# A fifth room for expert weights, and all of an octet's gathers in one pair: one buffer of gathered tokens in place of two

## The reference, cut to what matters

```
s = sigmoid(x @ router_w)                     # 64 experts, 8 chosen per token
shared = (silu(x @ sw1) * (x @ sw3)) @ sw2    # one shared expert for all tokens
for each expert e, on the tokens that chose it:
    xe = x[tok]                               # gather
    h  = silu(xe @ w1[e]) * (xe @ w3[e])      # 1024 -> 256, "gate" and "linear" product
    out[tok] += gate * (h @ w2[e])            # 256 -> 1024, "down" product, scatter
x = layer_norm(alpha * x + shared + out)
```

## Time and profile before

| | |
|---|---|
| median of 3 timed runs | 1344.71 us (1343.71 to 1345.81) |
| profiled execution | 1348.52 us, its span 1346.7 us |
| granted TensorE clock, mean | 0.999 |
| busy share of the span: PE, DVE, ACT, POOL | 97%, 35%, 23%, 6% |
| moved by DMA | 462.00 MB, mean 343 GB/s |
| chain that ended last | PE 77%, DMA 19%, DVE 2% |
| expert stage, layer 0 and layer 1 | about 178 to 637 us and 846 to 1304 us |

### The profile page before, as it was taken

The page is one execution under the profiler, slowest core; times in us unless marked ns, Lnnn a source line. Parts: engine busy times, 40 slices in busy tenths (PEclk is TensorE's granted clock), DMA queues, the critical chain, the costliest instruction groups (busy, mean ns, idle before and its releaser), DMA issues.

```text
span 1346.7 us, 23086 instructions
## 1 busy us (share of the span) xinstructions
PE 1303.1 (97%) x9730; PEld 750.1 (56%) x9730; DVE 475.4 (35%) x791; ACT 310.7 (23%) x747; POOL 81.0 (6%) x93
## 2 busy tenths in 40 slices
PE   9999999999999899998999999999999999999998
PEld 4555665555555455554498457555555545555544
DVE  1584532333332323323511246232332323333344
ACT  1244322121221221111210234222222221112112
POOL 2443100000000000000100021000000000000000
PEclk9999999999999999999999999999999999999999
DMA  9820679999999999999764527799999999999992
GB/s 305 305 97 32 250 299 419 420 420 421 421 421 420 421 420 422 420 420 385 244 229 147 196 96 278 309 419 421 419 420 421 420 421 421 421 421 421 420 382 78
DMA packets 83151, 462.00 MB, mean 343 GB/s; under 512 B 7024, under 2 KB 7504, under 8 KB 34672
## 3 DMA queue, kind: packets, MB, share of 16 engines
q1 hardware_dynamic: 81040, 454.15, 83.4%
q0 software_dynamic: 2016, 6.43, 1.6%
HBM read 459.50 MB, written 1.05 MB: 342 GB/s over the span
## 4 chain that ended last, share of the span: by engine, by line
PE 77%; DMA 19%; DVE 2%; issue 1%; ACT 0%; POOL 0%; SPq 0%; DVEq 0%; POOLq 0%
PE ps L1259 26%; DMA ring<-in_exp_w_dram 19%; PE ps L1299 12%; PE ps L918 4%; PE ps L1452 4%; PE ps L1321 4%; PE ps L1198 4%; PE ps L1095 3%; PE ps L1022 3%; PE ps L1167 2%; PE ps L1119 2%; PE ps L1269 1%; PE ps L1159 1%; PE ps L1080 1%; PE ps L1431 1%; PE ps L938 1%
## 5 line engine op out<-in xcount | busy, mean ns | idle before, releaser
L1299 PE MATMUL ps<-ring,qkT 128*32 128x512 f32 x1984 | 232.9, 595 | 4.1 <-issue 3.1
L2176 DVE TENSOR_TENSOR o_tok<-ps,o_tok 128x1024 f32<-128x1024 f32 x124 | 150.6, 1223 | 157.4 <-PE ps L1321 157.4
L2181 DVE TENSOR_TENSOR y_lo<-ps,y_hi 128x1024 fp32r<-128x1024 f32 x62 | 75.9, 1224 | 213.7 <-ACT y_hi L1684 213.7
L1259 PE MATMUL ps<-ring,xT 128*64 128x256 f32 x1008 | 124.5, 385 | 15.8 <-DMA ring<-in_exp_w_dram 15.8
L1299 PEld LDWEIGHTS ps<-ring,qkT 128*32 128x32 f32 x1984 | 61.5, 109 | 128.8 <-issue 128.3
L1259 PE MATMUL ps<-ring,pT 128*64 128x256 f32 x992 | 124.3, 385 | 6.7 <-DMA ring<-in_exp_w_dram 6.5
L1659 ACT ACTIVATE roped<-ps 128x256 f32<-128x256 f32 x64 | 24.6, 385 | 456.5 <-PE ps L1259 456.5
L1259 PE MATMUL ps<-ring,proj 128*64 128x256 f32 x1008 | 121.8, 379 | 0.0
L1259 PE MATMUL ps<-ring,gb_row 128*64 128x256 f32 x992 | 121.6, 379 | 0.0
L2165 DVE SCALAR_TENSOR_TENSOR roped<-roped,rows,ps 128x256 f32<-128x256 f32 x64 | 30.8, 481 | 237.4 <-ACT roped L1659 237.4
L1259 PEld LDWEIGHTS ps<-ring,xT 128*64 128x64 f32 x1008 | 71.0, 136 | 74.5 <-issue 34.6
(11 more groups left out here) (308 smaller groups left out, 1469.5 us busy)
## 6 DMA issues: line engine op xcount, KB each, us to landing
ring<-in_exp_w_dram SPq DMA_DIRECT2D x158, 2048.0 KB, 23.3
ring<-in_exp_w_dram SPq DMA_DIRECT2D x54, 1024.0 KB, 9.0
ring<-in_od_w_in_dram SPq DMA_DIRECT2D x6, 2048.0 KB, 8.6
ring<-in_ple_w_gate_dram SPq DMA_DIRECT2D x4, 2048.0 KB, 15.3
ring<-in_ev_w_in_dram SPq DMA_DIRECT2D x3, 2048.0 KB, 19.5
ring<-in_ev_w_o_dram SPq DMA_DIRECT2D x2, 2048.0 KB, 10.0
x_tok<-in_exp_w_dram SPq DMA_DIRECT2D x4, 1024.0 KB, 8.5
ring<-in_exp_w_dram SPq DMA_DIRECT2D x8, 512.0 KB, 15.9
```

The costliest lines, as they stand in the source:

```text
L1259: ins = pe.matmul(ps[b * SLOTS:(b + 1) * SLOTS, 2, w * FE:(w + 1) * FE], xe(odd, c)[:, u * P + b * SLOTS:u * P + (b + 1) * SLOTS], views[b ...
L1299: ins = pe.matmul(ps[q:q + TILE_SLOTS, 4 + half, :], hT[:, f, h0:h0 + TILE_SLOTS], down_rows(b, f, half), start=(f == 0), stop=(f == 1))
L2176: dve.tensor_tensor(ys, ps[:, bank:bank + 2, :], ys, ALU.add).then_inc(sem("y_added"), 1)
L2181: dve.tensor_tensor(y_lo[:, :], ps[:, 4:6, :].rearrange("p b n -> p (b n)"), y_hi[:, :], ALU.subtract)\
```

## The change

- **One buffer of gathered tokens** (`xe`, in `xT` and `pT`). All four gathers for the next octet stand in the octet's last pair: the first before the linear product, the second before the down product, the third between its halves, the fourth behind it. The first copy waits for the linear product that reads the old tokens last.
- **Rooms for experts.** What came free makes a permanent fifth room (`FIFTH`, the old extra room), and there is a sixth, used once in a layer, for expert 1 (`APART`: w1 in o_tok, w3 in qkT, w2 in gb_row). Six experts are loaded before the first pair ends. `home(e)` is the room of expert e, `room_of(e)` the expert whose room it takes; for e above 8 that is e - 5. Every expert has DMAs of its own; those of the fifth room's w2 are in three pieces.
- **PSUM.** The linear product has bank 3 and the gate product bank 2; `silu` waits for the gate product alone, `gate_h` also for the linear one.
- **y_acc** lies over expert 1's w1, so it is started on GpSimd after the first gate product, from x_hi + x_lo, in four operations, and not on ScalarE ahead of the experts.
- **Shared products** stand in pairs 24, 25, 26 and 28 (`SHARED_AT`).
- **The start**: two products with zeros go, and chunk 3 of tile 0 comes behind tile 1's transposes.
- `ple_pT` lies in p_tok; several semaphores are merged into `cmp_pe` and `fox_act`.

The core of the diff:

```diff
+FIFTH = RING
+APART = RING + 1
+EARLY_HOMES = (3, APART, 1, 2, FIFTH)
+CYCLE = (0, 3, 1, 2, FIFTH)
+SHARED_AT = (PAIRS - 8, PAIRS - 7, PAIRS - 6, PAIRS - 4)
+def home(e):
+    return EARLY_HOMES[e] if e < len(EARLY_HOMES) else CYCLE[e % len(CYCLE)]
+def room_of(e):
+    return {6: 0, 7: 2, 8: 3}.get(e, e - len(CYCLE))
...
+            def pair_load(L, m):
+                after = [e for e in range(6, NE) if room_of(e) // 2 == m]
+                whole = [e for e in after if e < NE - 2]
+                sp.wait_ge(sem("exp_gate"), L * PAIRS + m + 1)
+                for e in after:
+                    gate_load(L, e)
+                sp.wait_ge(sem("exp_up"), L * PAIRS + m + 1)
+                for e in whole:
+                    lin_load(L, e)
...
+                sp.wait_ge(sem("exp_down"), L * PAIRS + m + 1)
+                for e in whole:
+                    down_load(L, e)
...
+            def fifth_load(L):
                 sp.wait_ge(sem("router_mm"), NT * (L + 1))
                 sp.wait_ge(sem("x_split"), NT * (L + 1))
-                sp.wait_ge(sem("y_begun"), NT * (L + 1))
...
+                gate_load(L, 4)
+                sp.wait_ge(sem("shared_w1_used"), L + 1)
+                lin_load(L, 1)
+                sp.wait_ge(sem("gb_used"), NT * (3 * L + 1))
+                down_load(L, 1)
+                sp.wait_ge(sem("shared_h"), NT * (L + 1))
+                down_load(L, 4, (1,))
...
                     if k == e0 + 2:
+                        apart_gate_load(L)
                         shared_load(L)
+                        lin_load(L, 4)
+                        down_load(L, 4, (0,))
...
+                pool.wait_ge(sem("exp_gate"), L * PAIRS + 1)
+                for t in range(NT):
+                    step(pool.tensor_tensor(y_acc[:, t, :].rearrange("p (n c) -> p n c", c=DC),
+                                            x_hi[:, t, :].rearrange("p (c n) -> p n c", c=DC),
+                                            x_lo[:, t, :].rearrange("p (c n) -> p n c", c=DC), ALU.add))
+                    pool.tensor_scalar(y_acc[:, t, :], y_acc[:, t, :], ALPHA, None, ALU.mult).then_inc(sem("y_begun"), 1)
...
                         transpose_tile(x_tok, 0)
-                        multiply_zeros(2)
-                        wait_tile("xT", 3 * L, 0)
+                        wait_chunk(3 * L, 0, 0)
...
-                        chunks(0, 2, 4)
+                        chunks(0, 2, 3)
                         pe.wait_ge(sem("x_loaded1"), 16)
                         transpose_tile(x_tok, 1)
+                        chunks(0, 3, 4)
...
+                def pe_step(m, o, u, gather_next=True, selT_next=True, scatter_last=True):
                     par = u % 2
+                    gathers = gather_next and u == 3
+                    if m + M0 > 0:
+                        pe.wait_ge(sem("exp_h"), m + M0)
+                    if m > 0:
+                        pe.wait_ge(sem("selT_copied"), m + (M0 + 1))
+                    exp_up(m, o, u, 0)
+                    if scatter_last:
                         scatter(m - 1, 0, 1 - par)
+                    if m in SHARED_AT:
+                        shared_down(SHARED_AT.index(m))
+                    if gathers:
+                        gather(o + 1, 0)
+                    exp_up(m, o, u, 1)
+                    if scatter_last:
+                        if m in SHARED_AT:
+                            pe.wait_ge(sem("shared_added"), 4 * L + SHARED_AT.index(m) + 1)
+                        scatter(m - 1, 1, 1 - par, bank=6 if gathers else 0)
                     h_transpose(m)
                     if selT_next:
                         sel_transpose(m + 1, o + 1 if u == 3 else o, (u + 1) % 4)
+                    if gathers:
+                        pe.wait_ge(sem("xe_copied"), 4 * o + (4 * O0 + 5))
+                        gather(o + 1, 1)
+                    exp_down(m, 0, by_half=not selT_next)
+                    if gathers:
+                        pe.wait_ge(sem("xe_copied"), 4 * o + (4 * O0 + 6))
+                        gather(o + 1, 2)
+                    exp_down(m, 1, by_half=not selT_next)
+                    if gathers:
+                        pe.wait_ge(sem("xe_copied"), 4 * o + (4 * O0 + 7))
+                        gather(o + 1, 3)
...
```

More of the change, by code:

```diff
@@ new lines, in ffn_load, with last_lin_load @@
+            def ffn_load(L, e):
+                gate_load(L, e)
+                lin_load(L, e)
+                down_load(L, e)
+            def last_lin_load(L):
+                s, e = home(NE - 2), NE - 2
+                for half in range(2):
+                    cols = slice(half * UP_N // 2, (half + 1) * UP_N // 2)
+                    sp.dma_start(ring[:, s:s + 2, UP_N + cols.start:UP_N + cols.stop],
+                                 a["exp_w3"][L, e:e + 2].rearrange("e (p c) f -> p e (c f)", c=DC)[:, :, cols])\
+                      .then_inc(w_loaded[s + half], 16)
@@ new lines, in last_down_load @@
+            def last_down_load(L):
+                s, e = home(NE - 2), NE - 2
+                for half in range(2):
+                    cols = slice(half * PIECE, (half + 1) * PIECE)
+                    for b in range(2):
+                        w2 = ring[:, s + b, DOWN0:DOWN0 + 2 * D].rearrange("p (c f) -> p c f", c=2)
+                        sp.dma_start(w2[:, :, cols], a["exp_w2"][L, e + b].rearrange("(p c) f -> p c f", c=2)[:, :, cols])\
+                          .then_inc(down_loaded[s + half], 16)
@@ L565, in _ @@
+                    if k == e0 + RING:
+                        fifth_load(L)
+                        for m in range(PAIRS - 2):
+                            pair_load(L, m)
                         k = e0 + NE
@@ L1347, in pe_step @@
                         sel_transpose(m + 1, o + 1 if u == 3 else o, (u + 1) % 4)
-                    if own_gather and not scatter_last:
-                        gather(o + 1, u, halves=(1,))
-                    if inside:
-                        scatter(m - 1, 1, 1 - par)
-                    exp_down(m, par, first and M0 == 0, by_half=not selT_next)
-                    if late:
-                        pe.wait_ge(sem("xe_copied"), 4 * O0 + 7)
-                        gather(1, 3)
+                    if gathers:
[9 more added lines that the diff above has]
+                        gather(o + 1, 3)
                 pe.wait_ge(sem("x_split"), NT * (L + 1))
@@ L2227, in dve_step @@
                         y_low(m)
[L2228 removed]
+                    if gather_next and u == 2:
                         sel_bf_build(o + 1)
```

480 lines of the change are left out of this document (185 added, 295 removed).

## The result

The changed kernel took 1359.90 us (median of 5, 1359.74 to 1369.27) against 1345.81 (median of 5, 1343.71 to 1347.92): ratio 1.012, 95% interval 1.0098 to 1.0141. It is slower: the medians lie 14.1 us or 1.05% apart, and the ratio, in which every execution counts, says 1.2%. 1342.5 was forecast, and the range ended at 1350.

The account below looks back on a forecast made before the run. Weight stream and TensorE's chain were taken to bound the kernel side by side. Front -0.9, two layers at -1.0 each, +0.7 for handoffs make -2.2 us: 1342.5 us from a median of 1344.71, range 1337 to 1350.

Parts of the forecast that it names:

- The bound now, and the stream: Expert stages: weight stream at its limit, TensorE nearly as full; head start 3.3 us, less 2.0 a layer for smaller pieces.
- the 388 of the rival: Expert weight stream: small DMAs slow it to 388 GB/s, 31 us a layer, 1405 us in all; chance 0.03.
- The second stays at 1.02: Pair without a gather: handoff from h's transposes through ScalarE's copy to the down product stays 1.02 us.
- The gather pair, 17.2 forecast: Octet's last pair with all four gathers takes 17.2 us on TensorE.
- The last copy ... I cost them at nothing: Gather pair: ScalarE's copies of gathered chunks, 1.0 us each, lie hidden under TensorE's work and cost nothing.
- 1.91 forecast: Expert stage: each shared product adds 1.91 us to its pair on TensorE.
- the 457.1 forecast: TensorE's whole expert stage, summed over its octets, takes 457.1 us if no weights are late.
- The stage ends at 623.1 + 13.2: Pair 31's gate weights land at 623.1, then 13.2 us of work: end 636.3, not 637.3, so -1.0 a layer.
- slower, the serial chain decides: Every pair is a serial engine chain; 0.13 us more in each of 64 pairs gives +6, 1350.9 us; chance 0.20.
- The bound set beside it, 0.07 a pair: Serial chain in the expert stages: 0.07 us more at each of 64 pairs turns the forecast into slower.
- The signs: Wrong if pairs take 13.4 or more, stream below 410 GB/s, gather pairs over 17.6, or VectorE waits on GpSimd at pair 1.
- The front: Kernel start: two zero products go and a tile 0 chunk fills a TensorE wait, -0.9 us once; late y_acc up to 3 us hides.

Follow-up runs that it names:

- e_waits: Changed kernel with TensorE's two down-weight waits moved ahead of the second scatter half and the repeated y_split wait left out: 1359.51 us, ratio 1.010.
- e_waits_late: e_waits with the two down-weight waits behind the second scatter half, right ahead of h's transposes: 1362.17 us, ratio 1.0129.
- e_order_only: Changed kernel with expert weights loaded in the order of need from pair 7 on, nothing else: 1366.82 us, ratio 1.015.
- e_chain: Kernel before with the new order of TensorE work and second PSUM bank alone, keeping its rooms, loads and token buffers: 1358.44 us, ratio 1.0087.
- e_best2: Changed kernel, down-weight waits moved, loads by need, p's and first selection's transposes moved, early gate steps in pairs 4-14 and 24-26: 1345.36 us, ratio 0.9995.
- e_silu: Changed kernel with SiLU waiting for the linear product again, as before the change: 1390.92 us, ratio 1.0337.

## Why the prediction was wrong

**The bound now, and the stream: right.** The lead of the weights at 582 us is 1.6 us, 1.3 forecast. The single MiB DMAs and the pieces cost 2 GB/s of 421, nothing like the 388 of the rival. The page of the Trainium skill that was weighed ("DMA: Bandwidth & Descriptors", Bandwidth) gives its 78% of peak for single DMAs of 1 MB. Here a long queue of 1 MiB DMAs ran at 419 GB/s, against 421 with 2 MiB ones, so that rule did not describe this stream. (The fixed 2 us that the prediction quotes with it stands on the same page, in the section on the anatomy of one DMA.)

**"The second stays at 1.02": wrong, and the largest term.** This is the step that failed first. It took 1.18 us, in 23 or 24 pairs a layer, 4 us. The rows of before have three waits ahead of the down product, and the new kernel has four, since each expert's weights have a semaphore of their own. The forecast let signals cost 0.12 and put TensorE's own additional waits at nothing (its 0.01 a pair was for SP and VectorE). After's own trace shows the size: pair 31, with three waits, took 1.03 and layer 0's pair 0, also with three, 1.07. e_waits took the cost away (0.98), and e_waits_late brought it back at another place.

**The gather pair, 17.2 forecast, 17.49 measured,** in 7 pairs, 2.0 us: a gather ahead of another step takes 1.15 each time, not 1.07, and half a down product 1.85, not 1.79.

**"The last copy ... I cost them at nothing": wrong once a layer.** Behind pair 27 stand the transposes of p, not a gate product, and they waited 1.1 us. The chain was followed for an ordinary octet only. A shared product costs 2.0 in its pair (15.35 - 13.34), 1.91 forecast: VectorE, which also adds the shared product, takes up h 0.28 behind the linear product's end there (532.39 to 532.67) and not 0.18 (300.51 to 300.69), 0.4 us in four pairs.

These make 7.5 (4 + 2.0 + 1.1 + 0.4) of the 7.6 us by which the stage on TensorE (464.7) exceeds the 457.1 forecast.

**"The stage ends at 623.1 + 13.2": the step that hid a second error.** Weights and chain were added up only at pair 31. In between, the weights of an odd expert come 5.0 us later in the stream than they did, which is why e_waits gained nothing. In after itself nothing waits for them, so this cost is not part of the 14 us. It is what would have stopped the gain that a shorter chain was to bring, and in e_waits it did.

**The rival "slower, the serial chain decides" was the right one** (chance 0.20): it asked for 0.13 us more a pair and gave +6; with 0.16 a pair, the gather pairs and p's transposes it is +14. It stood at too low a chance, and at half its size. The bound set beside it, 0.07 a pair, was also a little small: 64 x 0.07 - 2.2 is 2.3 us, less than the 2.7 that count as a change.

**The signs were too coarse.** Pairs took 13.33 where 13.4 was to say wrong, gather pairs 17.49 where 17.6 was: 14 us were lost without either. The one sign of wrong that did appear, VectorE waiting on GpSimd at pair 1, cost nothing, as the text on the front had said of up to 3 us.

**The front.** 0.9 us forecast, 0.3 gained in the trace. Two of the first rows of after:

```profile
4.46 1.53 PE L720 MATMUL ps<-const,x_tok 128*128 128x128 f32 x8
7.68 2.81 PE L938 MATMUL ps<-ring,xT 128*128 128x512 f32 x6 [1.69 <-DMA ring<-in_ev_w_in_dram]
```

The zeros had covered a wait for the first weights, 1.69 us now. The products of the earlier trace rows end 0.3 us earlier (the next line starts at 22.62, before at 22.95). One trace doesn't settle the size: with the same front that line starts at 22.82 in e_waits, with a like wait, and at 21.80 in e_order_only, without one. Layer 0's first gate product stands at 178.46, where 177.8 was forecast; the selection's transposes wait for the third chunk's copy, as forecast.

**What stays open.** Whether in e_waits the weights would have been late with the waits at the product itself. The shares in the 14 us rest on one or two traces of each kernel: the order of work is 8.8 us in the stages of e_chain, and the rest fits the fourth wait, but no run of after took that wait away alone. No run tried the five rooms with the gathers spread out as before. Why a wait whose semaphore has passed costs time at all no run shows.

## What to carry over

In this kernel a wait in front of an instruction that stands right behind a handoff was not free, even on a semaphore long past: count the waits of the engine that is on the path, and put those that must be there behind work that covers them, unless what they wait for may be late. A deeper ring with an odd number of rooms is only a head start if the loads are also issued in the order of need: compare byte positions in the stream for each wait, not only at the end. Packing movable work into one place takes its cover away everywhere else: here a pair without its piece of 1.07 us got only 0.46 shorter (13.79 to 13.33), so each piece had hidden about 0.6 us. The room that this freed did not win that back: the best kernel with it, e_best2, is as fast as before.

## What the runs showed of the hardware

Waits on TensorE that find their semaphores already passed cost time where they stand right at a handoff. With four waits (the handoff's own among them) ahead of the down product, it starts 1.18 us behind h's transposes; with three 1.02 to 1.07, with one 0.98. Ahead of h's transposes two waits give 0.71 us from the linear product's end, three 0.76 (pair 31 of e_waits_late), four 0.91. So in both places the fourth costs about 0.15 us, and the one or two before it 0.04 to 0.09 together. In e_waits the same two waits on down weights stand ahead of the second scatter half, and the step behind it stays at 0.71: there they cost nothing.

In layer 1 of after, TensorE stands still in the first products behind the branch on the overflow flag. Timeline, then windows (columns as in the earlier trace rows; the last three are clock, DMA share, GB/s):

```profile
1319.61 1.13 PE L1412 MATMUL ps<-ring,p_tok 128*128 128x512 f32 x2
1325.57 8.34 PE L1412 MATMUL ps<-ring,p_tok 128*128 128x512 f32 x14 [4.84 <-issue]
```

```profile
1310.00:1318.00 8.00, 7.48 (x64) 3.40 (x62) 2.60 (x4) 1.08 (x3) 0.00 (x0) 1.00 0.95 341
1318.00:1326.00 8.00, 3.12 (x11) 1.10 (x10) 6.84 (x13) 1.99 (x3) 0.00 (x0) 0.81 0.73 262
1326.00:1334.00 8.00, 8.00 (x17) 3.32 (x17) 3.89 (x7) 0.00 (x0) 0.00 (x0) 0.77 0.00 2
```

It waits 4.84 us for nothing that the profile shows, and the granted clock falls from 1.00 to 0.81 and 0.77 in the two windows that hold the pause and what follows; in the 8 us behind them it is 1.00 again. The lower of the two levels is 1.2 GHz; a mean of 0.8 is some 3 of 8 us at it. Layer 0 of the same execution has neither. e_chain has a stall of 3.6 us at the same place in layer 0, e_silu one of 4.49 in layer 1, and behind both the clock fell as well (0.83 and 0.63 in 8 us). The other traces have none of this size. A transfer of the instruction queue (q8) lies about 3 us behind the first of these products, but e_waits has it at the same distance and no stall. Its cause was not tried.
